# Down projections of a hybrid encoder layer: products in another order, weight sums on VectorE, norm steps moved

## What is computed

```python
# x: (1, 1024, 1024) float32, D_FF = 2752
def swiglu(h, w_gate, w_up, w_down):
    return (jax.nn.silu(h @ w_gate) * (h @ w_up)) @ w_down

x = x + 0.5 * rmsnorm(swiglu(rmsnorm(x, g_ffn1_pre), w1_gate, w1_up, w1_down), g_ffn1_post)
h = rmsnorm(x, g_mix_pre)
z = h @ w_in                      # pool channels, q, k, v
mix = concat(pool_mixer(z), attention_mixer(z)) @ w_out
x = x + rmsnorm(mix, g_mix_post)
x = x + 0.5 * rmsnorm(swiglu(rmsnorm(x, g_ffn2_pre), w2_gate, w2_up, w2_down), g_ffn2_post)
```

## Time and profile before

| | us |
|---|---|
| median of 3 runs | 1853.21 (1851.71 to 1856.65) |
| the profiled execution: its own time | 1849.15 |
| its span, first to last instruction | 1847.3 |
| PE busy | 1747.6 (95%), granted clock 0.979 of full |
| DVE busy | 1086.6 (59%) |
| ACT busy | 704.0 (38%) |
| POOL busy | 751.3 (41%) |

### The profile page before, as it was taken

One profiled execution on the slowest core, in us unless ns is written; L12 is line 12 of the kernel. 1 busy time (PEld: TensorE's weight loads), 2 busy tenths in 40 slices (PEclk: granted clock), 3 DMA queues, 4 the chain that ended last, 5 costly groups with the idle time before them and its releaser, 6 DMA issues.

```text
span 1847.3 us, 21920 instructions
## 1 busy us (share of the span) xinstructions
PE 1747.6 (95%) x8062; PEld 1420.0 (77%) x8062; DVE 1086.6 (59%) x1309; ACT 704.0 (38%) x1218; POOL 751.3 (41%) x579
## 2 busy tenths in 40 slices
PE   4999999999899989999999998499999999999997
PEld 3788888887688867887888786378888888778886
DVE  5665556654545585433556657666556655464578
ACT  4423333232243543433444546333323333234443
POOL 6564545543354240117010201745445544254435
PEclk7999999999999999999999999799999999999999
DMA  4124232241953353433110156123232332384362
GB/s 160 46 87 141 92 109 86 88 140 58 320 159 94 115 175 103 126 105 91 46 58 24 53 165 199 63 69 125 89 105 86 106 128 84 125 279 148 94 202 103
DMA packets 155738, 214.64 MB, mean 116 GB/s; under 512 B 8752, under 2 KB 94960, under 8 KB 155632
## 3 DMA queue, kind: packets, MB, share of 16 engines
q1 hardware_dynamic: 148352, 186.96, 31.8%
q10 hardware_dynamic: 6288, 23.07, 3.5%
q0 software_dynamic: 992, 3.21, 0.5%
HBM read 161.17 MB, written 52.04 MB: 115 GB/s over the span
## 4 chain that ended last, share of the span: by engine, by line
PE 80%; DVE 7%; POOL 4%; DMA 3%; ACT 3%; issue 3%; ACTq 0%; SPq 0%; POOLq 0%; DVEq 0%
PE ps L1771 14%; PE ps L1769 14%; PE ps L1770 14%; PE ps L1828 6%; PE ps L1829 6%; PE ps L1830 6%; PE ps L1858 4%; PE ps L1860 4%; PE ps L1859 4%; PE ps L1968 2%; PE ps L2076 1%; PE ps L2078 1%; PE ps L2077 1%; PE ps L1936 1%; DMA st_op<-hd_dram 1%
## 5 line engine op out<-in xcount | busy, mean ns | idle before, releaser
L1769 PE MATMUL ps<-xg,ring 128*128 128x512 f32 (+1 forms) x1232 | 488.2, 396 | 19.1 <-DVE ring L1033 8.2
L1771 PE MATMUL ps<-xg,ring 128*128 128x512 f32 (+1 forms) x1232 | 486.9, 395 | 0.0
L1770 PE MATMUL ps<-xg,ring 128*128 128x512 f32 (+1 forms) x1232 | 484.2, 393 | 0.0
L1769 PEld LDWEIGHTS ps<-xg,ring 128*128 128x128 f32 (+1 forms) x1232 | 230.6, 187 | 74.5 <-DVE ring L1033 11.8
L1770 PEld LDWEIGHTS ps<-xg,ring 128*128 128x128 f32 (+1 forms) x1232 | 230.7, 187 | 55.4
L1771 PEld LDWEIGHTS ps<-xg,ring 128*128 128x128 f32 (+1 forms) x1232 | 230.4, 187 | 54.5
L1828 PE MATMUL ps<-ring 128*128 128x512 f32 (+1 forms) x616 | 243.4, 395 | 13.0 <-DVE ring L1045 12.6
L1829 PE MATMUL ps<-ring 128*128 128x512 f32 (+1 forms) x616 | 241.4, 392 | 0.0
L1830 PE MATMUL ps<-ring 128*128 128x512 f32 (+1 forms) x616 | 240.8, 391 | 0.0
L634 ACT ACTIVATE ring<-t_sum 128x512 fp32r<-128x512 f32 (+1 forms) x176 | 109.2, 621 | 316.5 <-PE ps L1771 190.4
L1042 DVE TENSOR_TENSOR ring<-st_op,ring 128x1024 fp32r<-128x1024 f32 (+1 forms) x110 | 143.1, 1302 | 124.3 <-ACT ring L645 124.3
(11 more groups left out here) (181 smaller groups left out, 2645.5 us busy)
## 6 DMA issues: line engine op xcount, KB each, us to landing
st_op<-hd_dram SPq DMA_DIRECT2D x140, 256.0 KB, 2.6
raw<-in_w_gate_dram SPq DMA_DIRECT2D x20, 1024.0 KB, 6.5
raw<-in_w_up_dram SPq DMA_DIRECT2D x20, 1024.0 KB, 5.4
raw<-in_w_in_dram SPq DMA_DIRECT2D x40, 512.0 KB, 3.8
hd_dram<-u_b SPq DMA_DIRECT2D x60, 256.0 KB, 6.4
raw<-in_w_out_dram SPq DMA_DIRECT2D x24, 512.0 KB, 3.5
hd_dram<-hst SPq DMA_DIRECT2D x40, 256.0 KB, 6.5
hd_dram<-u_a SPq DMA_DIRECT2D x40, 256.0 KB, 6.5
```

The source lines that it names most:

```text
L1769: pe.matmul(acc, hi[:, a, :], x_hi, start=(a == 0 and not more), stop=False, skip_group_check=more)
L1770: pe.matmul(acc, hi[:, a, :], x_lo, start=False, stop=False, skip_group_check=more)
L1771: mm = pe.matmul(acc, lo[:, a, :], x_hi, start=False, stop=(a == HALF_D - 1), skip_group_check=more)
```

## The change

The seven products run in the order P5, P7, P4, P3, P1, P2, P6 instead of P5, P4, P7, P3, P1, P2, P6; for this the h operands in DRAM and the evictions change places, and C21 takes P7 with a minus sign and then the bank of both. All sums of w_down move from GpSimd to VectorE: those of products 1 to 3 (counted from 0) into `st_op` four steps ahead as before, those of products 4 and 6 in place (`t_ahead`), over B21 in product 2 and over B12 in steps 39 to 49, so that these products read a plain block. SP loads B21 alone at the start, B11 in steps 11 to 17 and B12 in steps 20 to 26. GpSimd's loads of the gains wait for step 22. The tables of the norm steps change.

```diff
--- before.py
+++ after.py
 B11, B12, B21, B22 = range(4)
-T_DOWN = [(B22,), (B21, "-", B11), (B21, "+", B22), (B12, "-", B22), (B11, "+", B22), (B11,), (B11, "+", B12)]
+T_DOWN = [(B22,), (B21, "+", B22), (B21, "-", B11), (B12, "-", B22), (B21,), (B11,), (B12,)]
...
+AHEAD = {4: 0, 6: 1}
-H_OF = (7, 1, 8, 0, 4, 5, 6)
+H_OF = (7, 8, 1, 0, 4, 5, 6)
-ACT_EVAC = [((C11, -1.0), (C12, 1.0)), ((C21, 1.0),), (), ((C22, 1.0),), (), (), ()]
-DVE_EVAC = [(), (), ((C11, "+"),), ((C12, "+"),), ((C11, "+"),), ((C21, "+"), (C22, "-")), ((C22, "+"),)]
+ACT_EVAC = [((C11, -1.0), (C12, 1.0)), ((C21, -1.0),), (), ((C22, 1.0),), (), (), ()]
+DVE_EVAC = [(), (), ((C11, "+"), (C21, "+")), ((C12, "+"),), ((C11, "+"),), ((C21, "+"), (C22, "-")), ((C22, "+"),)]
...
-SQ1_AT, Z_AT, NEW_AT, SQ2_AT, NORM_AT = (0, 1, 2, 3), (2, 4, 7, 10), (3, 5, 8, 13), (4, 6, 9, 14), (6, 9, 15, 19)
-TURN_AT, TURN_BANK, LO_AT, EVAC_AT = (13, 16, 19, 21), (4, 4, 6, 4), (14, 18, 20, 21), (11, 12, 16, 17)
+SQ1_AT, Z_AT, NEW_AT, SQ2_AT, NORM_AT = (0, 1, 2, 3), (2, 4, 6, 9), (3, 5, 7, 10), (4, 6, 8, 11), (6, 8, 10, 13)
+TURN_AT, TURN_BANK, LO_AT, EVAC_AT = (13, 14, 16, 18), (4, 6, 4, 6), (14, 15, 17, 19), (11, 12, 12, 13)
...
+        def plain_ready(eng, p, q, j):
+            if q in AHEAD:
+                eng.wait_ge(ahead_done, PAIRS * (2 * p + AHEAD[q]) + j + 1)
+            else:
+                wd_ready(eng, p, T_DOWN[q][0], j)
...
                 sp.wait_ge(used, end)
-                for g in (0, 1, 2):
+                for g in (0, 1):
                     load_down(p, B21, g)
-                    load_down(p, B11, g)
                 store_h(p, PAIRS - 1)
                 for d in range(ST, D_STEPS):
                     load_operand(p, d)
-                    if d in (6, 8):
-                        load_down(p, B21, 3 + (d - 6) // 2)
-                        load_down(p, B11, 3 + (d - 6) // 2)
-                    if d in (16, 18, 20, 24, 28):
-                        load_down(p, B12, (16, 18, 20, 24, 28).index(d))
+                    if d in (6, 7, 8):
+                        load_down(p, B21, d - 4)
+                    if d in (11, 12, 13, 15, 17):
+                        load_down(p, B11, (11, 12, 13, 15, 17).index(d))
+                    if d in (20, 21, 22, 24, 26):
+                        load_down(p, B12, (20, 21, 22, 24, 26).index(d))
...
-                    wd_ready(act, p, T_DOWN[q][0], j)
+                    plain_ready(act, p, q, j)
...
-                            act.wait_ge(t2_done, D_SUMS * p + SUM_AT[5] * PAIRS)
+                            act.wait_ge(t2_done, D_SUMS * (p + 1))
+                            act.wait_ge(ahead_done, PAIRS * (2 * p + 1))
...
+            def t_down(p, d):
...
+                dve.tensor_tensor(st_op[0:pw, d % ST, HALF:D], wd_block(x, j)[0:pw, :], wd_block(y, j)[0:pw, :],
+                                  ALU.add if op == "+" else ALU.subtract).then_inc(t2_done, 1)
+
+            def t_ahead(p, q, j):
+
+                pw, dst = PW[j], wd_block(T_DOWN[q][0], j)
+                x, y = (B11, B22) if q == 4 else (B11, B12)
+                dve.wait_ge(t2_done, D_SUMS * p + SUM_AT[2 if q == 4 else 3] * PAIRS + j + 1)
+                wd_ready(dve, p, x, j)
+                wd_ready(dve, p, y, j)
+                dve.tensor_tensor(dst[0:pw, :], wd_block(x, j)[0:pw, :], wd_block(y, j)[0:pw, :], ALU.add)\
+                   .then_inc(ahead_done, 1)
+
             def down(p):
...
-                    if q in (3, 4) and j < HT:
-                        evac(p, q - 1, j)
+                    if d + 4 < D_STEPS and len(T_DOWN[(d + 4) // PAIRS]) == 3:
+                        t_down(p, d + 4)
+                    if q == 2:
+                        t_ahead(p, 4, j)
+                    if 0 <= d - 39 < PAIRS:
+                        t_ahead(p, 6, d - 39)
+                    if q == 3 and j % 2 == 0 and j < 2 * HT:
+                        evac(p, 2, j // 2)
+                    if q == 4 and j < HT:
+                        evac(p, 3, j)
...
-            def t_down(p, d):
...
             def down(p):
 
                 pool.wait_ge(h_out, 16 * PROD * PAIRS * (p + 1))
+                pool.wait_ge(lo_done, D0[p] + 2 * PAIRS)
...
                 for d in range(D_STEPS):
-                    if d + 4 < D_STEPS and len(T_DOWN[(d + 4) // PAIRS]) == 3:
-                        t_down(p, d + 4)
                     e = d - 5 * PAIRS
...
                 elif q < Q_MIX + HT:
-                    if i in (1, 3):
-                        pe.wait_ge(xlo_done, x_number(Q_MIX) + (i + 1) // 2)
+                    if i >= 2:
+                        pe.wait_ge(xlo_done, x_number(Q_MIX) + i - 1)
```

More of the change, by code:

```diff
@@ L309, in layer_program @@
         t2_done = sem("t2_done")
+        ahead_done = sem("ahead_done")
         y_act = sem("y_act")
@@ L1215, in evac @@
                     dve.tensor_tensor(y, y, m, ALU.add if sign == "+" else ALU.subtract).then_inc(y_dve, 1)
+            def t_down(p, d):
+                q, j = divmod(d, PAIRS)
+                if d >= ST:
+                    dve.wait_ge(lo_done, D0[p] + d - ST + 1)
+                x, op, y = T_DOWN[q]
+                wd_ready(dve, p, x, j)
+                wd_ready(dve, p, y, j)
+                pw = PW[j]
+                dve.tensor_tensor(st_op[0:pw, d % ST, HALF:D], wd_block(x, j)[0:pw, :], wd_block(y, j)[0:pw, :],
[4 more added lines that the diff above has]
+                dve.wait_ge(t2_done, D_SUMS * p + SUM_AT[2 if q == 4 else 3] * PAIRS + j + 1)
+                wd_ready(dve, p, x, j)
+                wd_ready(dve, p, y, j)
+                dve.tensor_tensor(dst[0:pw, :], wd_block(x, j)[0:pw, :], wd_block(y, j)[0:pw, :], ALU.add)\
+                   .then_inc(ahead_done, 1)
             def down(p):
@@ L1541, in gate_up @@
                 h_sums(p, PAIRS - 1)
-            def t_down(p, d):
[L1544 to L1548, removed]
-                wd_ready(pool, p, y, j)
-                pw = PW[j]
-                pool.tensor_tensor(st_op[0:pw, d % ST, HALF:D], wd_block(x, j)[0:pw, :], wd_block(y, j)[0:pw, :],
-                                   ALU.add if op == "+" else ALU.subtract).then_inc(t2_done, 1)
             def down(p):
                 pool.wait_ge(h_out, 16 * PROD * PAIRS * (p + 1))
+                pool.wait_ge(lo_done, D0[p] + 2 * PAIRS)
                 if p == 0:
```

## The result

The changed kernel takes **1826.91 us** (median of 4 runs, 1822.17 to 1827.46) against 1852.46 us for the kernel before (4 runs, 1851.24 to 1856.65), a ratio of 0.9852 with an interval of 0.983 to 0.9875. The forecast was 1828, range 1821 to 1842. Against the medians the gain is 25.5 us; between the two profiled executions it is 21.7 us (1849.15 to 1827.46), where the sum of terms said 25.6. The two differ because the profiled execution of before lay 3.3 us under its median here, and that of after 0.5 us above its own. The terms are therefore judged on the traces.

What follows compares the result with a forecast made beforehand. The tensor engine was taken to bound nearly everywhere, so only its waits could be saved: 7.7 + 4.4 - 1 + 8.2 + 5.4 + 0.9 = 25.6 us off 1849.15 gives 1823.6, plus 4.1 for the median: 1828 us, range 1821 to 1842.

Steps and rivals of the forecast that it cites:

- Starts, 11.1 us: Start of both down projections: fewer bytes ahead of operand loads remove the waits, 7.7 us and 4.4 us, less 1.
- The operand that I expected late (-1): At the stage starts: one operand load may still be late, taking 1 us off the gain.
- The price of a wait: Tensor engine waits: each costs 0.16 us more than printed, as a matmul shows 0.39 us but the next starts after 0.23.
- Sums on VectorE cost nothing: Both stages: 55 sums moved to VectorE at 0.60 us each stay hidden by matmuls.
- The rival of VectorE as the bound: Products 2 and 3: dearer sums make the tensor engine wait; 1856 us at 1.30 a sum, 1910 at 1.98; chance 0.12.
- the waits of 1.8 us: First stage's tail: two waits, 2.1 us with 0.16 each, put down to GpSimd's sums lengthening low halves; they would go.
- Tail, 8.2 us: End of first stage: 2.1 us of waits and 7.9 at the first turning go, less a new wait of 1.8.
- The low half starts 1.3 us into a step: VectorE's adding up for the first stage's tail: step 13's low half start, a plain one taken 0.1 us later.
- the 0.8 for the turning: First turning: its 1.62 us halves at full clock, 0.8 us less.
- Input projection, 5.4: Before the input projection: the wait of 3.67 + 0.16 us goes, and the slow clock behind it; 5.4 us.
- the second stage's end, 0.9: Late in the second down projection: waits of 0.4 and 0.2 us go, with 0.16 each; 0.9 us.

Runs made afterwards that it cites:

- e5: The changed kernel with B11 and the gains both loaded as early as in the kernel before; 1838.66 us, ratio 0.9929.
- e3: The changed kernel with B11 loaded as early as before, interleaved with B21, the gains staying late; 1831.78 us, ratio 0.9898.
- e7: The changed kernel with three more unread 128x512 sums on VectorE in each step of product 1; 1839.29 us, ratio 0.9934.
- e2: The kernel before with its 55 sums of a stage on VectorE at the same steps, nothing else changed; 1845.41 us, ratio 0.9969.
- e8: The changed kernel with all 55 sums of a stage back on GpSimd, at the changed kernel's places; 1827.97 us, ratio 0.9876.
- e12: The changed kernel with ScalarE's store, load and squares of tile 0 one step later, behind the operand's high part; 1822.14 us, ratio 0.9829.
- e1: The changed kernel with the norm, turning and eviction tables of the kernel before; 1828.38 us, ratio 0.9876.
- e9: The changed kernel with evictions in the first stage's last product one step earlier; 1823.1 us, ratio 0.9844.

## Why the prediction was right, and where not

- **Starts, 11.1 us: right in cause, a little small.** e5, which undoes just this, loses 11.8 by the medians and 13.8 in the stages. The operand that I expected late (-1) was not. The cause as given, bytes ahead of the operand loads, is shown by e3 to e5, and that it isn't additive I had not seen. The price of a wait was 0.27 us more than printed, not 0.16, because the second matmul behind it starts 0.34 us after the first, not 0.23 (at 494.61 and 499.25 in the kernel before); over ten waits that is 1.1 us.
- **Sums on VectorE cost nothing: right, by 0.60 us each.** Product 2, with two sums in a step, has no wait, and e7 shows what lies beyond the limit: with four the step is as long as VectorE's own list, 3.55 us. The rival of VectorE as the bound fell with that price.
- **Why the sums should leave GpSimd: only half right.** I took the waits of 1.8 us and part of the turning's to come from the engine of the sums. e2 agrees, where the sums keep their late places and only the engine changes. But e8 shows that the engine counts only there: early on GpSimd costs no more than 1.7 us over early on VectorE. Not run by itself is the new order of the products, which makes the early sums possible.
- **Tail, 8.2 us: the mis-sized term.** The step that failed is "The low half starts 1.3 us into a step", taken over to e = 5. It held in product 1, and did not where ScalarE issues a store and a load and squares a tile ahead of the high part. Measured against the sum: the wait was 3.83 + 0.16 = 4.0 for 1.8 (2.2 more), the 0.8 for the turning did not come, and the four starts behind it (668.75 to 670.58) took 1.83 us for 0.92 at full clock, 0.9 more. Together 3.9 us of the 8.2, so 4.3 came. e12 removes nearly half of the wait by moving one ScalarE step, and with it the lower clock.
- **Input projection, 5.4, and the second stage's end, 0.9: the waits right, 1.6 us not seen in the sum.** None of these waits is in the trace, and e1 brings the first back (3.66 us). The lower clock behind it, 1.6 us of the 5.4, is gone too, but it lies in the stretch between the stages, and that one is as long as before (906.84 for 906.89). The three kernels with the lower clock there average 907.4 us, the other eleven 906.0, so the 1.6 us is likely real and was hidden by the spread of that part.
- **The 21.7 us** between the profiled executions, stretch by stretch. To the input projection the terms say 7.7 + 8.2 + 3.8 = 19.7; less 3.9 for the tail, plus 0.6 for the dearer waits, that is 16.4, and 16.5 was measured. In the second stage they say 4.4 + 0.9 = 5.3, or 5.9 with the dearer waits, and 6.3 was measured. Between them 1.6 was due and nothing came. Against all this stands 1.1 us at the start: the stage of the changed kernel begins at 476.87 us instead of 475.76, though the change leaves TensorE's work up to there as it was. I did not trace that; over the kernels run here this start lies between 474.3 and 477.6 us, so I take it as spread between executions.
- That the median came within 1.1 us of the forecast is partly luck. The profiled execution fell 3.9 us short of the sum, and the forecast had added 4.1 us because the profiled run of before lay under its median; that of after lay 0.5 us above its own.

## To carry to other kernels

When a step's work on one engine is added up, start it where the engine it waits for really lets it start in that step: side work that is queued ahead of the producer (an issue of a transfer, a reduction) counts as much as work on the engine itself. Bytes ahead of an urgent load cost less while there is slack than when it is gone (2.1 us for the gains alone, 5.4 on top of B11), so undo such parts singly and together. Compare stretches that begin at the same instruction, since the time of a whole execution carries the spread of all its other parts. Before moving work to another engine, try moving it in time on the one it has.

## What was not expected of the hardware

GpSimd's two tiny operations for the reciprocal root (128x1) take 0.19 and 0.55 us when VectorE is idle (643.60) or reads PSUM (the same again at 663.60, beside the evictions), and much longer beside VectorE's work with two SBUF inputs. Kernel after, GpSimd:

```profile
643.60 0.19 POOL L1508 TENSOR_SCALAR ms<-ss 128x1 f32<-128x1 f32 x1 [3.86 <-ACT junk_d L723]
643.87 0.55 POOL L1510 TENSOR_TENSOR r<-ms,neg_half 128x1 f32<-128x1 f32 x1
649.29 2.58 POOL L1508 TENSOR_SCALAR ms<-ss 128x1 f32<-128x1 f32 x1 [4.87 <-ACT junk_d L723]
651.95 2.67 POOL L1510 TENSOR_TENSOR r<-ms,neg_half 128x1 f32<-128x1 f32 x1
```

The second pair made the norm of tile 1 wait 0.44 us.

In the two stages of these runs, and at the input projection, the granted clock fell to its lower level (starts 0.43 us apart) behind waits of 1.90 us (e2, first stage), 2.39 (e9), 2.59 (before and e5), 2.65 (e2, second stage) and all those of 3.66 and more. It did not behind 1.80 (e1, turning), 2.12 (before, second stage), 2.15 (e12), 2.23 (e3, second stage) and 2.96 us. The last is the first turning of e7:

```profile
673.49 1.09 PE L1753 MATMUL ps<-ident,y 128*128 128x128 f32 x8 [2.96 <-DVE y L1227]
674.34 0.48 PE L1865 MATMUL ps<-ring 128*128 128x512 f32 x1
```

So the length of the wait alone does not say whether the clock falls: 1.90 and 2.39 us did it and 2.96 did not. A shorter wait can give back more than its own length, as in e12, and in e9 it did not.
